# Paged attention of the sampled tokens moved into the loop over pairs of heads, with the pages first copied by pair in DRAM

## The reference, cut to what matters

```
def trunk(x, p, ...):                     # once for the prompt, once for the sampled tokens
    x = short_conv_layer(x, ...)          # x + W_out(silu(z) * B * conv3(C * x_in)), h @ w_in_a: 1024 x 4096
    x = x + sigmoid(x @ w_ple_gate[0]) * (p[0] @ w_ple_proj[0])
    k, v, logf = shared_kv(x, ...)        # rmsnorm, h @ w_kv: 1024 x 2064
    q, z = split(rmsnorm(x) @ w_in_b, 2)
    x = x + (attend(q) * silu(z)) @ w_out_b
    x = x + sigmoid(x @ w_ple_gate[1]) * (p[1] @ w_ple_proj[1])
    return rmsnorm(x), ...
prompt:  s[t,u] = q_t.k_u/8 + c[t] - c[u], causal, c = cumsum(logf); softmax(s) @ v
k_past = cache_k[page_table].reshape(8, 1024, 16, 64)          # 8 pages per sequence; v_past, logf_past likewise
sampled: s_past = q.k_past/8 + cn[t] + rest[u],  s_new = q.k_new/8 + cn[t] - cn[u], causal
         softmax(concat(s_past, s_new)) @ concat(v_past, v_new)
```

## Time and profile before

| | us |
|---|---|
| median of 3 runs (lowest, highest) | 1923.3 (1920.9, 1925.4) |
| the profiled execution, its own time | 1923.05 |
| its span, first to last instruction | 1921.3 |
| PE / DVE / ACT / POOL busy in the span | 1766.8 / 888.1 / 692.3 / 265.5 |
| moved by DMA | 161.6 MB |

### The profile page before, as it was taken

One profiled execution on the slowest core, in us unless ns is written; L12 is line 12 of the kernel. 1 busy time (PEld: TensorE's weight loads), 2 busy tenths in 40 slices (PEclk: granted clock), 3 DMA queues, 4 the chain that ended last, 5 costly groups with the idle time before them and its releaser, 6 DMA issues.

```text
span 1921.3 us, 33244 instructions
## 1 busy us (share of the span) xinstructions
PE 1766.8 (92%) x11874; PEld 1617.0 (84%) x11874; DVE 888.1 (46%) x1433; ACT 692.3 (36%) x1150; POOL 265.5 (14%) x233
## 2 busy tenths in 40 slices
PE   6999999999999769999999999999779999899997
PEld 5999999999999659888888888888656666699997
DVE  4433333343253474555555555555444344423443
ACT  5111111121142234565655556555423233302332
POOL 4111111100000022222212222221100000000010
PEclk8999999999999889999999999999869999899998
DMA  4111111111211213110102111010326868721102
GB/s 140 46 46 45 45 45 45 45 33 44 75 42 30 104 13 103 35 57 23 56 23 78 46 34 56 24 56 23 134 94 268 304 258 329 279 75 49 41 27 93
DMA packets 163427, 161.61 MB, mean 84 GB/s; under 512 B 18188, under 2 KB 140172, under 8 KB 163126
## 3 DMA queue, kind: packets, MB, share of 16 engines
q1 hardware_dynamic: 163382, 161.03, 25.3%
HBM read 137.20 MB, written 23.80 MB: 84 GB/s over the span
## 4 chain that ended last, share of the span: by engine, by line
PE 74%; DVE 9%; ACT 5%; issue 5%; DVEq 3%; ACTq 2%; POOL 1%; DMA 0%; SPq 0%; POOLq 0%
PE PS L577 14%; PE PS L579 14%; PE PS L578 14%; PE PS L738 4%; PE PS L740 4%; PE PS L739 3%; PE PS L797 3%; PE PS L844 3%; PE PS L785 2%; DVE small L1505 2%; PE PS L911 2%; PE PS L768 2%; PE PS L866 2%; DVE pTl L1516 1%; PE PS L769 1%
## 5 line engine op out<-in xcount | busy, mean ns | idle before, releaser
L577 PE MATMUL PS<-Hhi,w_hi 128*128 128x364 f32 (+1 forms) x1536 | 511.9, 333 | 38.3 <-DVE Hlo L1351 35.1
L579 PE MATMUL PS<-Hhi,w_lo 128*128 128x364 f32 (+1 forms) x1536 | 509.7, 332 | 0.0
L578 PE MATMUL PS<-Hlo,w_hi 128*128 128x364 f32 (+1 forms) x1536 | 507.3, 330 | 0.0
L577 PEld LDWEIGHTS PS<-Hhi,w_hi 128*128 128x128 f32 x1536 | 293.9, 191 | 42.5 <-issue 29.1
L578 PEld LDWEIGHTS PS<-Hlo,w_hi 128*128 128x128 f32 x1536 | 293.1, 191 | 0.0
L579 PEld LDWEIGHTS PS<-Hhi,w_lo 128*128 128x128 f32 x1536 | 292.7, 191 | 0.0
L738 PE MATMUL PS<-Hhi,w_hi 128*128 128x364 f32 (+1 forms) x768 | 274.0, 357 | 0.1
L740 PE MATMUL PS<-Hhi,w_lo 128*128 128x364 f32 (+1 forms) x768 | 252.6, 329 | 0.0
L739 PE MATMUL PS<-Hlo,w_hi 128*128 128x364 f32 (+1 forms) x768 | 251.9, 328 | 0.0
L991 ACT ACTIVATE w_hi<-w_raw 128x1024 fp32r<-128x1024 f32 (+1 forms) x97 | 105.7, 1090 | 371.3 <-PE PS L579 368.1
L504 POOL TENSOR_TENSOR w_raw<-w_raw,GT 128x1024 f32<-128x1024 f32 x65 | 127.1, 1957 | 697.9 <-DMA w_raw<-in_w_kv 386.3
(11 more groups left out here) (254 smaller groups left out, 2303.4 us busy)
## 6 DMA issues: line engine op xcount, KB each, us to landing
Kpages<-in_cache_k SPq DMA_DIRECT2D x64, 512.0 KB, 5.8
Vpages<-in_cache_v SPq DMA_DIRECT2D x64, 512.0 KB, 5.6
w_raw<-in_w_in_a SPq DMA_DIRECT2D x64, 256.0 KB, 3.0
w_raw<-in_w_ple_gate SPq DMA_DIRECT2D x16, 512.0 KB, 3.7
w_raw<-in_w_kv SPq DMA_DIRECT2D x32, 256.0 KB, 3.2
w_raw<-in_w_in_b SPq DMA_DIRECT2D x32, 256.0 KB, 3.2
parked_x<-X SPq DMA_DIRECT2D x8, 544.0 KB, 5.0
X<-parked_x SPq DMA_DIRECT2D x8, 544.0 KB, 7.8
```

Of the source, the lines that this page charges most:

```text
L577: mm(out, wh, hi[:, k, s:e], start=(k == 0), stop=False)
L578: mm(out, wh, lo[:, k, s:e], start=False, stop=False)
L579: last = mm(out, wl, hi[:, k, s:e], start=False, stop=(k == nk - 1))
```

## The change

The same products and the same softmax, in another order and layout:

- **Copies in DRAM.** In the convolution stage, beside each page's log forget values, SP also issues two DMAs from DRAM to DRAM: the page of keys into `keys_by_pair` and the page of values into `values_by_pair`. Each moves 512 KB as 128 rows x 8 pieces of 512 bytes (one piece for each pair of heads). There are 128 of them, 67 MB in all.
- **A key phase after half 0 and a value phase after half 1 of each pair.** A pair now serves all 8 sequences at once: 8 loads ("units") of keys and 8 of values, 512 KB each, pass through `ring`, which has three places. The 128 PSUM rows of the scores are 8 sequences x 2 heads x 8 tokens, all used. The bias comes as two matmuls over 50 rows (`Ar`, and `KA` filled by the DMAs of `load_bias`).
- **The dense pieces are dealt out anew**: 40 to half 0, 12 to the key phase, 38 to half 1, 6 to the value phase (`half_steps`, `KEY_D`, `VALUE_D`) in place of 48 and 48.
- **Memory.** `KT` and `PsT` are now parts of `Pb`, the probabilities' buffer; `SS`, the sampled scores, lies in PSUM banks 5 to 7, which the transposes of probabilities also use. The weights' buffers have chunk and parity swapped, so that their tails, which the attention loop doesn't use, can hold small operands.
- **The old phase after the loop is gone.** The parked outputs of 7 pairs are fetched during the last half.

```diff
-STEPS = [("S", 0), ("D", 2), ("N", 0), ("N", 1), ("D", 1), ("S", 1), ("D", 2), ("N", 2), ("D", 1), ("S", 2), ("D", 3),
-         ("S", 3), ("D", 3), ("S", 4), ("D", 4), ("T", 0, 0), ("T", 0, 1), ("S", 5), ("D", 5), ("V", 0, 0), ("T", 0, 2),
...
+def half_steps(first, turns, last):
+    behind = dict(zip(range(7), first))
+    steps = []
+    for qb in range(8):
+        steps += [("S", qb)]
+        if qb < 7:
+            n = behind[qb]
+            if qb == turns[0]:
+                steps += [("D", n), ("N", 0), ("N", 1), ("D", 1)]
+            elif qb == turns[1]:
+                steps += [("D", n), ("N", 2), ("D", 1)]
+            else:
+                steps += [("D", n)]
+        else:
+            steps += [("D", last[0]), ("V", 0, 2), ("D", last[1]), ("V", 0, 3), ("D", last[2]), ("T", 1, 0), ("T", 1, 1)]
+        steps += {4: [("T", 0, 0), ("T", 0, 1)], 5: [("V", 0, 0), ("T", 0, 2)], 6: [("V", 0, 1), ("T", 0, 3)]}.get(qb, [])
+    for kb in range(8):
+        steps += [("D", 1), ("V", 1, kb)] + ([("T", 1, kb + 2)] if kb < 6 else [])
+    return steps
+HALF0 = half_steps((2, 1, 2, 2, 3, 4, 5), (0, 1), (6, 1, 4))
+HALF1 = half_steps((2, 1, 2, 2, 3, 4, 5), (1, 2), (5, 1, 3))
+KEY_D = [1, 1, 2, 1, 2, 1, 2, 2]
+VALUE_D = [2, 4]
 TURN_PARTS = [(0, 1, 2, 3), (4, 5, 6), (7, 8)]
...
+        ring = sb(es, "ring", [P, RING, D])
...
+        KT = Pb[:, 0:2 * D].rearrange("p (u g n) -> p u g n", u=2, g=4)
+        PsT = Pb[:, 2 * D:2 * D + 9 * P].rearrange("p (t n) -> p t n", n=P)
...
+        dk = nc.dram_tensor("keys_by_pair", (NPAIR, 4 * P + 1, DB, 2, P), F32, kind="Internal").ap()
+        dv = nc.dram_tensor("values_by_pair", (NPAIR, 8 * P + 1, DB, P), F32, kind="Internal").ap()
...
+                            rows = page(j, pg)
+                            sp.dma_start(at_pair(LFP[:, pg], j).rearrange("p b h -> p (b h)"), cl[rows, :]).then_inc(sems["s_logf"], 16)
+                            by_pair = lambda x: x[rows, :].rearrange("t (j c) -> t j c", j=NPAIR)
+                            sp.dma_start(dk[:, pg // 2 * P:(pg // 2 + 1) * P, bass.ds(j, 1), pg % 2, :].rearrange("j t b c -> t j (b c)"),
+                                         by_pair(ck)).then_inc(sems["pages_in"], 16)
+                            sp.dma_start(dv[:, pg * P:(pg + 1) * P, bass.ds(j, 1), :].rearrange("j t b c -> t j (b c)"),
+                                         by_pair(cv)).then_inc(sems["pages_in"], 16)
...
+            def load_unit(j, u):
+                if u >= RING:
+                    if u - RING < PAGES:
+                        sp.wait_ge(sems["s_kturn1"], 8 * j + u - RING + 1)
+                    else:
+                        sp.wait_ge(sems["s_vused"], 8 * j + u - RING - PAGES + 1)
+                    sp.sem_inc(sems["sp_step"], 1)
+                pair = bass.ds(j, 1)
+                if u < PAGES:
+                    e, pp = u // 4, u % 4
+                    src = dk[pair, pp * P:(pp + 1) * P, :, :, :].rearrange("j t (g e) x c -> (j t) g e (x c)", e=2)[:, :, e, :]
+                    dst = ring[:, SLOT[u], :].rearrange("p (g c) -> p g c", g=4)
+                else:
+                    src = dv[pair, (u - PAGES) * P:(u - PAGES + 1) * P, :, :].rearrange("j t b c -> (j t) (b c)")
+                    dst = ring[:, SLOT[u], :]
+                sp.dma_start(dst, src).then_inc(sems[f"r_in{SLOT[u]}"], 16)
...
+            def keys(j, more):
+                for u in range(RING, PAGES):
+                    load_unit(j, u)
+                if more:
                     load_b1(j, 3, 1)
+                else:
+                    for u in range(2):
+                        load(N_B2 + u, (N_B2 + u) % 2, w_out_b[:, :, P * u:P * u + P])
+                for u in range(PAGES, PAGES + RING):
+                    load_unit(j, u)
...
+            def values(j, more):
+                for u in range(PAGES + RING, 2 * PAGES):
+                    load_unit(j, u)
+                if more:
+                    sp.wait_ge(sems["s_vused"], 8 * j + 8)
+                    sp.sem_inc(sems["sp_step"], 1)
+                    for u in range(RING):
+                        load_unit(j + 1, u)
...
+            def s_turn(j, u):
+                pe.wait_ge(sems[f"r_in{SLOT[u]}"], 16 * (USES[SLOT[u]] * j + USE[u] + 1))
+                for c in range(2):
+                    if u:
+                        pe.wait_ge(sems[f"s_kt{c}"], 8 * j + u)
+                    elif c == 0:
+                        pe.wait_ge(sems["exp"], START["exp"] + 16 * j + 8)
+                    for i in range(4):
+                        x = 4 * c + i
+                        last = tp(PS[:, 3 + c, i * P:(i + 1) * P], ring[:, SLOT[u], x * P:(x + 1) * P], ident[:, :])
+                    last.then_inc(sems[f"s_kturn{c}"], 1)
+            def s_bias(j):
+                pe.wait_ge(sems["bk_in"], 128 * j + 128)
+                pe.wait_ge(sems["kq_lo"], 3 * j + 3)
+                for c in range(2):
+                    mm(SS[:, 512 * c:512 * c + 512], Ar, KA[0:BIAS_ROWS, 0, 512 * c:512 * c + 512], start=True, stop=False)
+            def s_scores(j, u):
+                e, pp = u // 4, u % 4
+                for c in range(2):
+                    pe.wait_ge(sems[f"s_kt{c}"], 8 * j + u + 1)
+                for g_ in range(4):
+                    last = mm(SS[32 * g_:32 * g_ + 32, 256 * pp:256 * pp + 256], qc[:, g_, e, :], KT[:, u % 2, g_, :],
+                              start=False, stop=(e == 1 and pp % 2 == 1))
+                last.then_inc(sems["s_score"], 1)
+            def s_new(j):
+                pe.wait_ge(sems["o_free"], START["o_free"] + 4 * j + 2)
+                mm(SS[:, KEYS:], Ar, Bn, start=True, stop=False)
+                for e in range(2):
+                    for g_ in range(4):
+                        last = mm(SS[32 * g_:32 * g_ + 32, KEYS:], qc[:, g_, e, :], knT, start=False, stop=(e == 1))
+                last.then_inc(sems["s_all"], 1)
+            def key_phase(j, more):
+                q = Q_KEYS
+                s_bias(j)
+                for u in range(PAGES):
+                    s_turn(j, u)
+                    if u:
+                        s_scores(j, u - 1)
+                    dense(j, q, KEY_D[u], more)
+                    q += KEY_D[u]
+                s_scores(j, PAGES - 1)
+                s_new(j)
+            def value_phase(j, more):
+                pe.wait_ge(sems["exp"], START["exp"] + 16 * j + 16)
+                pe.wait_ge(sems["s_exp"], j + 1)
+                for c in range(2):
+                    for x in range(4):
+                        last = tp(PS[:, 3 + c, x * P:(x + 1) * P], Ps[:, (4 * c + x) * P:(4 * c + x + 1) * P], ident[:, :])
+                    last.then_inc(sems["s_back"], 1)
+                tp(PS[0:NS, 5, 0:P], Ps[:, KEYS:], ident[:, :]).then_inc(sems["s_back"], 1)
+                dense(j, Q_VALUES, VALUE_D[0], more)
+                pe.wait_ge(sems["s_pt0"], 2 * j + 2)
+                for pg in range(PAGES):
+                    if pg == 4:
+                        pe.wait_ge(sems["s_pt1"], j + 1)
+                    u = PAGES + pg
+                    pe.wait_ge(sems[f"r_in{SLOT[u]}"], 16 * (USES[SLOT[u]] * j + USE[u] + 1))
+                    for g_ in range(4):
+                        last = mm(PS[32 * g_:32 * g_ + 32, 6, 0:256], PsT[:, pg, 32 * g_:32 * g_ + 32],
+                                  ring[:, SLOT[u], 256 * g_:256 * g_ + 256], start=(pg == 0), stop=False)
+                    last.then_inc(sems["s_vused"], 1)
+                for e in range(2):
+                    for g_ in range(4):
+                        last = mm(PS[32 * g_:32 * g_ + 32, 6, P * e:P * e + P], PsT[0:NS, PAGES, 32 * g_:32 * g_ + 32], vnew, start=False, stop=(e == 1))
+                last.then_inc(sems["s_pv"], 1)
+                dense(j, Q_VALUES + VALUE_D[0], VALUE_D[1], more)
+                pe.wait_ge(sems["o_free"], START["o_free"] + 4 * j + 4)
+                pe.wait_ge(sems["s_osb"], j + 1)
+                tp(PS[:, 7, 0:P], Osb, ident[:, :]).then_inc(sems["s_yturn"], 1)
             for p in range(24, PIECES):
...
+            def key_phase(j, more):
+                q = Q_KEYS
+                for u in range(PAGES):
+                    act.wait_ge(sems["s_kturn0"], 8 * j + u + 1)
+                    if u >= 2:
+                        act.wait_ge(sems["s_score"], 8 * j + u - 1)
+                    af(KT[:, u % 2, 0:2, :].rearrange("p g n -> p (g n)"), PS[:, 3, :], ACT.Copy).then_inc(sems["s_kt0"], 1)
+                    dense(j, q, KEY_D[u], more)
+                    q += KEY_D[u]
+                act.wait_ge(sems["s_max"], j + 1)
+                af(Ps[:, :], SS, ACT.Exp, bias=small[:, 24:25], accum_out=small[:, 25:26])
+                act.drain().then_inc(sems["s_exp"], 1)
+            def value_phase(j, more):
+                act.wait_ge(sems["s_back"], 3 * j + 1)
```

(35 more changed lines are left out.)

569 lines of the change are left out of this document (211 added, 358 removed).

## The result

| | median us | lowest to highest | profiled span |
|---|---|---|---|
| before | 1922.1 | 1919.5 to 1925.4 | 1921.3 |
| changed | 2113.6 | 2111.2 to 2117.3 | 2111.8 |

The ratio is 1.0997, 95% interval 1.0973 to 1.1021. The change makes the kernel 10% slower; the forecast was 1902 us, within 1872 to 1990. It is wrong, and on both of its large terms.

What follows compares the result with a forecast made beforehand. PE's order of work was taken to bound the kernel. From 1923.05 us, the loop's 222 more against 244.6 removed gave -22.6, copies 0, small things +1: 1901.5, stated as 1902, range 1872 to 1990 for 8 in 10.

Steps and rivals of the forecast that it cites:

- both of its large terms: The loop with the sampled phase gone, put at -22.6 us, and the convolution stage's DRAM copies, put at 0.
- The copies in DRAM: Convolution stage: four copies per tile take 10.1 us of DMA time, fill the 12.0 with the weights, cost 0.
- The upper bound of 15.4: Convolution stage: copies pay read and then write, 15.4 us per tile, 17.3 with weights; upper end +155 us.
- The lower bound of 7.7: Convolution stage: copies cost what loads in 512-byte pieces cost, at most 7.7 us per tile, so nothing is late.
- the copies bind the convolution stage: Rival, the 32 convolution tiles: copies at 12.5 us per tile add 61 us, giving 1963; chance 0.33.
- The ring in the value phase: Value phase of each pair: PE waits for late value units, 6.0 us a pair, 48 for eight.
- The clock: Value phase: idle time lowers PE's granted clock, losing 1.7 us a pair, 14 for eight; ends 0 and twice that.
- The cover of the halves: Attention halves with 8 to 10 fewer dense pieces each: sum 0, ends of -2 and +4 us per pair.
- PE's own work: PE's new key, score, value, transpose and bias work in each pair: 19.3 us, 154 for eight.
- Key phase, exponential: Key phase: cost 0; PE's wait for maximum and exponential of the sampled scores: 0.8 us a pair, 6 for eight.
- The removed phase and the wait at the new end: After the loop: the sampled phase of 244.6 us goes; the 3.81 us wait before the next stage stays.

Runs made afterwards that it cites:

- the run with three units: The changed kernel with only the first three of each pair's eight value units loaded: 2033.5 us, a pair 110.6 us instead of 125.9.

## Why the prediction was wrong, step by step

- *The copies in DRAM*: the step that failed. I took 10.1 us per tile, by the load in pieces of the same size with a third on top, and from it a cost of 0; the stage's length gives 14.2 (115.3 + 16, over 32, is 4.1 above 12.0 - 1.9). The upper bound of 15.4, read and write both paid, was the nearer one, but by luck: a copy in whole rows also reads and writes every byte, and took 6.1. The lower bound of 7.7 comes close to the copies gathered in 512-byte pieces (7.3 to 7.7). Neither row was near to the operation: the load divides the read, and the store writes its pieces 4 KB apart, where the copy wrote them 4 MiB apart. The rival "the copies bind the convolution stage" is shown, with its mechanism and place; the 61 us taken for it were too few, the copies alone cost 110 and the stage lost 115.
- *The ring in the value phase*: the mechanism and the places were right, 6.0 forecast, 7.5 measured. The first wait was 4.64 us and not 2.4, since the load stands behind the pair's store (asked for 1.6 us into the phase, not 0.7) and takes 4.4 us to land, not 3.2.
- *The clock*: the second failure. I carried over 1.7 us a pair from the start of the stage behind. Taking the ring's waits away gave back 15.3 us a pair, 7.8 beyond the waits, and 7.5 of PE's busy time went with the granted clock's rise from 0.91 to 0.99; so the clock costs four to five times my figure. It reaches past the waits: five units at 1.08 us, and three dense pieces at half clock behind them.
- *The cover of the halves*: put at 0 with ends of -2 and +4. Their waits came to 8.2 us a pair against 4.3 before, +3.9. Putting most pieces back, with two more places for keys, gave 3.3 us a pair.
- *PE's own work*: 19.3 forecast. At full clock, as in the run with three units, the value products take 3.8, the transposes of keys 8.6, those of probabilities 1.3, the bias 1.0, the scores 30.7 of busy time in six pairs, 5.1. With the new values, new keys and the output that is some 2 us over the forecast.
- *Key phase, exponential*: 0 and 0.8 forecast; three waits of 0.5 us each in a pair (for the exponential, the copy to `KT` and the stage) make 1.5.
- *The removed phase and the wait at the new end*: right; the next stage begins 4.34 us behind the last transpose, 3.81 before.

The pair's miss is 13.6 us. Clock beyond forecast 6.1, ring 1.5, halves 3.9, small waits 0.7 and work up to 2 make 14; the busy times of overlapping matmuls don't close better than that.

## What to carry to other kernels

Before a copy from DRAM to DRAM is given to a stage for free, ask where its pieces are written: gathering in short pieces and writing in rows was cheap here, scattering the same pieces 4 MiB apart took nearly twice the DMA time, and the weights behind it in the one queue came late with it. Price an idle stretch of PE with the low clock that follows it; here each microsecond of waiting in the value phase cost two. And a load that comes late for lack of space may find space in a buffer that the same phase has just finished with.

## What the runs showed of the hardware

- A copy of 512 KB between DRAM tensors took 1.5 us of DMA time in rows of 4 KB, 1.8 written by 2 KB, 1.8 to 1.9 read by 512 bytes, 3.0 written by 1 KB, and 3.5 written by 512 bytes 4 MiB apart (keys 3.8, values 3.2). A store of 0.56 MB in pieces of 512 bytes, 4 KB apart, took 1.9.
- With the DMA share at 1.0, some issuing instructions took long: that of a page of values 0.57 to 7.98 us, median 3.31, and that of a weight load 0.50 to 3.94, median 2.08, where a page of keys took 0.61 and, in the kernel before, a weight load 0.39.
- The rate of the scattered copies moved between two runs of the same kernel: 187 GB/s (window 300 to 360) and 177, 26 us in the total, while the medians of the kernel before moved by about 3 us.
- Eight matmuls of 256 columns by 32 rows took 0.50 us, and 1.08 at the low clock.
